# A two-request attention encoder: in the 1024-token request, three heads of four are transposed by DMA instead of one of two, and every product with V stands two slots behind its head

## The chip, the cores and the metric

One core of one Trainium2 chip runs the whole program in one launch. The metric is the device time of that launch in microseconds; lower is better. The engines have these names here: PE is TensorE, DVE is VectorE, ACT is ScalarE, POOL is GpSimd, and SP is the queue (SyncE) from which all DMAs of this kernel are issued.

## What is computed

Two layers of a hybrid attention block, for two requests that share the weights: 512 tokens and 1024 tokens, 1024 channels wide.

```python
for l in range(2):                                   # layers
    shift, scale, gate = split(silu(c) @ w_ada[l] + b_ada[l])
    h = rms_norm(x) * (1 + scale) + shift
    q_lat, kv_lat, k_rope, z_a, q_b, k_b, v_b, z_b = split(h @ w_in[l])
    # group A: 8 heads of latent attention, q and k 96 wide, v 64 wide
    # group B: 8 query heads over 2 key heads, 64 wide, rotated by row and column
    ya = softmax(qa @ ka.T * s_a) @ va * silu(z_a)
    yb = softmax(qb @ kb.T * s_b) @ vb * silu(z_b)
    x = x + gate * (concat(ya, yb) @ w_out[l])
y = rms_norm(x)
```

There is no mask: in the 1024-token request every query row has 1024 scores in each of 16 heads.

## The kernel before

**Tiles and heads.** The program runs four instances one after the other (layer 0 with 512 tokens, layer 0 with 1024, then both of layer 1). An instance first makes all keys and values, then goes over tiles of 128 query tokens: `over_tiles` calls `tile(i, first, last)` on every engine, and a tile has 16 slots, one for each head `h`. The 1024-token instances have 8 tiles, i = 0 to 7. Only these instances are touched by the change.

**One head.** TensorE makes the scores (128 x 1024, two PSUM banks; `scores`). VectorE takes the row maximum (`row_max`), ScalarE the exponential into a row buffer of 32-bit numbers (`exponentials`, two such buffers, for even and odd heads). The product with V needs the probabilities with keys on the partitions, so they have to be transposed, and as two 16-bit parts (high, low) whose sum stands for the 32-bit number. There are two ways:

- by TensorE (odd heads before): `turn` makes 8 transposes of 128 x 128 into two PSUM banks, ScalarE copies each bank out as the high part and VectorE subtracts it from the bank for the low part (`move_pt` on either engine). The result lies in `PT_next`.
- by DMA (even heads before): ScalarE writes the high part of the rows and VectorE the low part (`row_low`) into one buffer `p_rows` of 128 x 2048 16-bit numbers, and SP issues one transposing DMA (`turn_rows`) into `PT`. In the profile `p_rows` has the name of the tile it lies in, `hT`, and `PT` and `probs` lie in `region`.

`mix(h)` is the product with V: 24 matmuls of 64 columns. SP issues the transposing DMA of head h only when the low part of its rows is there and when `mix(h - 2)` has read `PT` (`pv_done`).

**What sets the order.** Each engine runs its own program in the order in which it is written, and waits on semaphores. Besides the head's own steps a slot carries pieces of the projections, placed by hand in the tables `GATE_A`, `FINISH`, `OWN` and `PREPARE`: left of the bar a piece stands ahead of the products, right of it behind them. `"z_b/0"` and `"z_b/1"` are the halves of one projection.

```python
FINISH = [..., {2: "| y_b^T", 11: "| out0/0", 12: "out0/1 |", 13: "| out1/0", 14: "out1/1 |"}]
GATE_A = {0: "| z_a/0", 1: "z_a/1 |"}
OWN = [..., {2: "q_b^T0 |", 3: "| z_b/0", 4: "z_b/1 |", 5: "q_b^T1 |", 15: "| y_a^T"}]
PREPARE = [..., {6: "| q_lat", 7: "| q_b/0", 8: "q_b/1 | q_lat^T", 9: "q_up0 |", 10: "| q_up1", 12: "| q_a^T0", 14: "| q_a^T1"}]
```

All these pieces but `q_b^T0` go through one PSUM bank (`SIDE`), so a piece waits until VectorE has emptied the bank of the piece before it. In slot h TensorE makes the scores of head h + 2, ScalarE the exponential of head h + 1, VectorE the maximum of head h + 2 and the low part of head h + 1. TensorE's order in a slot is: `turn(h)` if h is odd; scores; the pieces left of the bar; in even slots `mix(h - 2)` and `mix(h - 1)`; the pieces right of the bar. VectorE's `outputs(0, i)` (heads 0 to 7 times the gate) stands in slot 8, `outputs(1, i - 1)` in slot 0 of the next tile. SP loads the next tile's rows of h (`load_h`) once `z_b` is done, behind the transposing DMA of head 4. ScalarE's sums of squares for `q_b` follow its work on head 10 in slot 9 (`query_squares`).

## Time and profile before

| | |
|---|---|
| median of 3 runs | 2256.93 us (2255.62 to 2258.09) |
| the profiled execution | 2250.96 us, its span 2248.9 us |
| granted TensorE clock, mean of the span | 0.967 |
| TensorE busy | 1983.3 us (88%) |
| VectorE busy | 1582.6 us (70%) |
| ScalarE busy | 1031.7 us (46%) |
| GpSimd busy | 844.0 us (38%) |
| the DMA queue's packets, share of 16 engines | 40.1% |

The profile is of one execution; its time is 6 us under the median of the runs, so a sum made from it is compared with 2250.96 us and then carried over. Busy shares are means over stages with different limits.

### The profile page before, as it was taken

The page shows a single profiled execution, that of the slowest core. Times are in us where ns is not written, and L with a number is a line of the kernel's source. Part 1 is how long each engine was busy: PE and PEld are TensorE (multiplying, and loading weights), DVE is VectorE, ACT ScalarE, POOL GpSimd, SP SyncE. Part 2 cuts the span into 40 slices and gives each one's busy share as a digit, 9 for nine tenths or more (in the row PEclk, how much of TensorE's full clock was granted, in tenths as well). Part 3 has the DMA queues.
Part 4 walks back from the last instruction along what each step waited for, and adds up shares of the span by engine and source line. Part 5 has one row for each costly group of instructions (what it writes and reads, how often), then busy time and mean ns, then how long its engine had stood idle before and what let it go on. Part 6 is the DMA issues. An engine that isn't in the chain of part 4 may idle for free.

```text
span 2248.9 us, 40514 instructions
## 1 busy us (share of the span) xinstructions
PE 1983.3 (88%) x15994; PEld 1173.9 (52%) x15994; DVE 1582.6 (70%) x2634; ACT 1031.7 (46%) x2110; POOL 844.0 (38%) x1343
## 2 busy tenths in 40 slices
PE   4889998898799999999868899889879999999987
PEld 1445554454456565655534555445446555556553
DVE  4668666586877777777736765748778777777774
ACT  1224345344655555555512434525365555555552
POOL 0663241385531233133136533218752343233320
PEclk7999999998999999999989999999999999999998
DMA  9812124552534443443562001246244334443443
GB/s 330 311 48 76 57 104 171 203 201 48 122 76 85 85 67 76 92 85 68 117 238 94 20 17 69 105 166 257 66 122 95 78 84 80 91 85 76 85 85 85
DMA packets 344752, 248.48 MB, mean 110 GB/s; under 512 B 273418, under 2 KB 299120, under 8 KB 344564
## 3 DMA queue, kind: packets, MB, share of 16 engines
q1 hardware_dynamic: 344566, 245.91, 40.1%
q8 instruction: 128, 2.10, 0.4%
q14 instruction: 58, 0.48, 0.1%
HBM read 130.50 MB, written 39.88 MB: 76 GB/s over the span
## 4 chain that ended last, share of the span: by engine, by line
PE 55%; DVE 20%; DMA 13%; ACT 6%; issue 2%; SPq 2%; POOL 1%; DVEq 0%; ACTq 0%; POOLq 0%
PE psum L737 27%; DMA region<-hT 9%; PE psum L728 6%; PE psum L730 6%; PE psum L729 6%; PE psum L719 5%; PE psum L968 4%; DVE nmax L1370 3%; DVE hT L1076 2%; DMA hT<-h_transposed 2%; DVE hT L1393 2%; DVE region L1386 2%; ACT junk L1487 1%; ACT hT L1619 1%; DVE region L1321 1%
## 5 line engine op out<-in xcount | busy, mean ns | idle before, releaser
L1370 DVE TENSOR_REDUCE nmax<-psum 128x1 f32<-128x1024 f32 (+1 forms) x384 | 399.1, 1039 | 19.2 <-PE psum L737 15.8
L719 PE MATMUL psum<-ident,region 128*128 128x128 f32 (+2 forms) x2200 | 311.0, 280 | 74.1 <-ACT region L1613 30.3
L719 PEld LDWEIGHTS psum<-ident,region 128*128 128x128 f32 (+2 forms) x2200 | 246.6, 141 | 127.2 <-issue 56.7
L1625 ACT ACTIVATE PT_next<-psum 128x512 f16<-128x512 f32 x256 | 140.7, 595 | 322.8 <-PE psum L719 322.5
L737 PE MATMUL psum<-KTa,region 96*128 96x512 f16 x960 | 249.3, 392 | 18.1 <-DVE region L1254 13.6
L1680 POOL TENSOR_TENSOR region<-region,rope_sb 128x64 f32<-128x64 f32 (+3 forms) x384 | 162.8, 445 | 271.3 <-DVE region L1326 261.3
L737 PE MATMUL psum<-Wq,hT 128*128 128x512 f32 (+1 forms) x512 | 202.6, 542 | 0.0
L1386 DVE TENSOR_TENSOR PT_next<-psum,PT_next 128x512 f16<-128x512 f32 x256 | 164.3, 683 | 50.1 <-ACT PT_next L1625 49.9
L728 PE MATMUL psum<-Wq,hT 128*128 128x512 f16 (+1 forms) x512 | 181.3, 354 | 17.4 <-DVE region L1339 10.1
L737 PE MATMUL psum<-KTb,region 128*128 128x512 f16 x640 | 171.5, 383 | 18.5 <-ACT xn L1613 13.1
L730 PE MATMUL psum<-Wq,hT 128*128 128x512 f16 (+1 forms) x512 | 180.9, 353 | 0.0
L729 PE MATMUL psum<-Wq,hT 128*128 128x512 f16 (+1 forms) x512 | 180.8, 353 | 0.0
L1487 ACT ACTIVATE junk<-region 128x64 bf16<-128x64 f32 (+3 forms) x300 | 87.5, 295 | 192.5 <-DVE region L1272 121.7
L1613 ACT ACTIVATE region<-psum,nmax,scalars 128x1024 f32<-128x1024 f32 (+1 forms) x128 | 126.4, 988 | 106.8 <-DVE nmax L1373 105.2
L1613 ACT ACTIVATE region<-psum,nmax,unscale 128x1024 f32<-128x1024 f32 (+1 forms) x128 | 126.1, 985 | 102.0 <-DVE nmax L1373 101.5
L1393 DVE TENSOR_TENSOR hT<-xn,hT 128x1024 f16<-128x1024 f32 x112 | 142.8, 1275 | 38.7 <-ACT hT L1619 36.6
L737 PE MATMUL psum<-region,hT 128*128 128x416 f32 x384 | 150.1, 547 | 20.0 <-DVE hT L1076 17.9
L1619 ACT ACTIVATE hT<-xn 128x1024 f16<-128x1024 f32 x112 | 118.5, 1058 | 101.8 <-DMA region<-hT 100.8
L1680 POOL TENSOR_TENSOR scalars<-scalars 128x1 f32<-128x1 f32 x32 | 6.1, 214 | 418.9 <-ACT region L1613 418.9
L737 PEld LDWEIGHTS psum<-KTa,region 96*128 96x128 f16 x960 | 92.7, 100 | 124.1 <-issue 29.8
L737 PEld LDWEIGHTS psum<-Wq,hT 128*128 128x128 f32 x512 | 93.6, 190 | 75.3 <-issue 71.7
L1321 DVE SCALAR_TENSOR_TENSOR region<-region,psum 128x512 f32<-128x512 f32 x48 | 33.0, 688 | 136.2 <-ACT region L1594 136.2
(202 smaller groups left out, 3883.1 us busy)
## 6 DMA issues: line engine op xcount, KB each, us to landing
w_in_parts<-parts SPq DMA_DIRECT2D x28, 512.0 KB, 2.8
Wq<-w_in_parts SPq DMA_DIRECT2D x16, 896.0 KB, 7.1
Wq<-in_w_in SPq DMA_DIRECT2D x6, 2048.0 KB, 14.9
hT<-h_transposed SPq DMA_DIRECT2D x24, 512.0 KB, 4.3
Va<-in_w_ada SPq DMA_DIRECT2D x12, 1024.0 KB, 5.5
Wout<-in_w_out SPq DMA_DIRECT2D x4, 2048.0 KB, 10.2
h_transposed<-parts SPq DMA_DIRECT2D x16, 512.0 KB, 2.9
Wout<-in_w_out SPq DMA_DIRECT2D x16, 512.0 KB, 4.9
```

Of the source, the lines that this page charges most:

```text
L719: return nc.tensor.transpose(out, in_, ident[0:n, 0:n])
L728: nc.tensor.matmul(out, rows[:, 0, k, :], high(k), start=k == 0, stop=False)
L729: nc.tensor.matmul(out, rows[:, 0, k, :], low(k), start=False, stop=False)
L730: last = nc.tensor.matmul(out, rows[:, 1, k, :], high(k), start=False, stop=k == KD - 1)
L737: last = nc.tensor.matmul(out, lhsTs[k], rhss[k], start=k == 0, stop=k == n - 1)
L1370: last = nc.vector.reduce_max(nmax[:, h:h + 1], scores_buf(h, S), AX_X, negate=True)
L1386: nc.vector.tensor_tensor(pt(h, S, 1, 4 * c)[:, 0:4, :], psum[:, turn_bank(S, h, c), :].rearrange("p (c n) -> p c n", c=4), pt(h, S, 0, 4 ...
L1393: nc.vector.tensor_tensor(p_rows[:, S:2 * S], probs_buf(h, S, i == NT - 1), p_rows[:, 0:S], ALU.subtract).then_inc(s["p_low"], 1)
L1613: nc.scalar.activation(probs_buf(h, S, i == NT - 1), scores_buf(h, S), ACT.Exp, bias=nmax[:, h:h + 1], scale=scale, accum_out=sums[:, h:h ...
L1619: nc.scalar.activation(p_rows[:, 0:S], probs_buf(h, S, i == NT - 1), ACT.Copy).then_inc(s["p_high"], 1)
L1625: nc.scalar.activation(pt(h, S, 0, 4 * c)[:, 0:4, :], psum[:, turn_bank(S, h, c), :].rearrange("p (c n) -> p c n", c=4), ACT.Copy).then_in ...
L1680: mul = lambda out, a, b: nc.gpsimd.tensor_tensor(out, a, b, ALU.mult)
```

## The change

In every tile of a 1024-token instance but the first (i > 0), the heads with h % 4 != 3 are transposed by DMA, 12 of 16; in the first tile it stays with the even heads. Even heads go into `PT`, odd ones into `PT_next`, and each has its own semaphore (`p_turned0`, `p_turned1`). The row buffers alternate between `p_rows` and half of `parts` (`rows_buf`), so ScalarE waits for the transposing DMA two back, not for the last one. TensorE makes `mix(h - 2)` in every slot: ahead of `turn(h)` where head h is TensorE's, else behind the scores and the pieces left of the bar. `outputs(0, i)` moves to the start of slot 9 and `outputs(1, i - 1)` to the start of slot 1 of the next tile.

```diff
+    def by_dma(r, i, h):
+        return r and (h % 4 != 3 if i else h % 2 == 0)
...
+        def rows_buf(h, i):
+            return parts[:, 0, :] if i and dma_heads(1, i, h) % 2 else p_rows
...
                     sp.wait_ge(s["p_low"], row_heads(q, i, h))
                     wait(sp, "pv_done", heads(b0, i, h - 2))
-                    sp.dma_start_transpose(PT[:, :, :, :].rearrange("p a c n -> p (a c) n"), p_rows).then_inc(s["p_turned"], 16)
+                    sp.dma_start_transpose((PT, PT_next)[h % 2][:, :, :, :].rearrange("p a c n -> p (a c) n"), rows_buf(h, i)).then_inc(s[f"p_turned{h % 2}"], 16)
...
-                        if r and h % 2 == 0:
+                        if by_dma(r, i, h):
                             turn_rows(h, i)
...
                     for h, (before_mix, after_mix) in enumerate(slots(first, last, q == 0, r)):
-                        if short or h % 2:
+                        late = not short and not first
+                        if late and not by_dma(r, i, h):
+                            mix(h - 2, i)
+                        if not by_dma(r, i, h):
                             turn(h, i)
...
-                        if not short and h % 2 == 0 and (h or not first):
+                        if late and by_dma(r, i, h) or not short and first and h % 2 == 0 and h:
                             mix(h - 2, i)
-                        if (short or h % 2 == 0) and (h or not first):
+                        if (short or first and h % 2 == 0) and (h or not first):
                             mix(h - 1, i)
...
-                            by_pe = h % 2
+                            by_pe = not by_dma(r, i, h)
+                            if not first and h == 1:
+                                outputs(1, i - 1)
+                            if not first and h == HEADS + 1:
+                                outputs(0, i)
...
-                    if r and h % 2 == 0:
+                    if by_dma(r, i, h):
 
                         act.wait_ge(s["exp_done"], heads(b0, i, h))
-                        wait(act, "p_turned", 16 * (row_heads(q, i, h) - 1))
-                        nc.scalar.activation(p_rows[:, 0:S], probs_buf(h, S, i == NT - 1), ACT.Copy).then_inc(s["p_high"], 1)
+                        k = dma_order.index((i, h))
+                        if k:
+                            wait(act, *rows_turned(q, *dma_order[k - 1 - (k > HEADS)]))
+                        if k == HEADS:
+                            act.wait_ge(s["out_moved0"], 16 * (KD // 2) * (l + 1))
+                        nc.scalar.activation(rows_buf(h, i)[:, 0:S], probs_buf(h, S, i == NT - 1), ACT.Copy).then_inc(s["p_high"], 1)
```

The order of instructions at three places shows what moves. All are of layer 0, 1024 tokens, in a tile from the middle; `psum<-Va,region` and `psum<-Vb,region` are products from `PT`, the same from `PT_next` are products from `PT_next`.

TensorE, from the products of slot 8 to the scores of slot 11, before: the products of heads 6 and 7, `q_lat^T` (2) and `turn(9)` (8) in one row, scores, `q_up0`, scores, the products of heads 8 and 9, `q_up1`, `turn(11)`, scores:

```order
L968 MATMUL psum<-Va,region 128x64 x24
L968 MATMUL psum<-Va,PT_next 128x64 x24
L719 MATMUL psum<-ident,region 128x128 x10
L737 MATMUL psum<-KTb,region 128x512 x4
L737 MATMUL psum<-Wuq,region 128x384 x2
L737 MATMUL psum<-KTb,region 128x512 x4
L968 MATMUL psum<-Vb,region 128x64 x24
L968 MATMUL psum<-Vb,PT_next 128x64 x24
L737 MATMUL psum<-Wuq,region 128x384 x2
L719 MATMUL psum<-ident,region 128x128 x8
L737 MATMUL psum<-KTb,region 128x512 x4
```

The same place now:

```order
L991 MATMUL psum<-Va,region 128x64 x24
L742 MATMUL psum<-ident,region 128x128 x2
L760 MATMUL psum<-KTb,region 128x512 x4
L760 MATMUL psum<-Wuq,region 128x384 x2
L991 MATMUL psum<-Va,PT_next 128x64 x24
L760 MATMUL psum<-KTb,region 128x512 x4
L991 MATMUL psum<-Vb,region 128x64 x24
L760 MATMUL psum<-Wuq,region 128x384 x2
L991 MATMUL psum<-Vb,PT_next 128x64 x24
L742 MATMUL psum<-ident,region 128x128 x8
L760 MATMUL psum<-KTb,region 128x512 x4
```

The 8 transposes of head 9 are gone and the four products stand in four slots, each two behind its head; `turn(11)` stays.

VectorE at the border of two tiles, before, from `outputs(1, i - 1)` in slot 0 to `y_b^T` of slot 2 (a `PT_next` row is `move_pt(1)`, the `xn,hT` row the low part of head 2, `nmax<-psum` a maximum):

```order
L1400 TENSOR_TENSOR region<-psum,region 128x512
L1386 TENSOR_TENSOR PT_next<-psum,PT_next 128x512 x2
L1370 TENSOR_REDUCE nmax<-psum 128x1
L1373 TENSOR_SCALAR nmax<-nmax,scalars 128x1
L1321 SCALAR_TENSOR_TENSOR region<-region,psum 128x512
L1237 TENSOR_REDUCE scalars<-region 128x1
L1393 TENSOR_TENSOR hT<-xn,hT 128x1024
L1333 CAST region<-psum 128x512
L1370 TENSOR_REDUCE nmax<-psum 128x1
L1373 TENSOR_SCALAR nmax<-nmax,scalars 128x1
L1338 CAST region<-psum 128x512
L1339 TENSOR_TENSOR region<-psum,region 128x512
```

The same place now, from the low part of head 1 in slot 0:

```order
L1419 TENSOR_TENSOR hT<-region,hT 128x1024
L1427 TENSOR_TENSOR region<-psum,region 128x512
L1396 TENSOR_REDUCE nmax<-psum 128x1
L1399 TENSOR_SCALAR nmax<-nmax,scalars 128x1
L1347 SCALAR_TENSOR_TENSOR region<-region,psum 128x512
L1263 TENSOR_REDUCE scalars<-region 128x1
L1419 TENSOR_TENSOR parts<-xn,parts 128x1024
L1359 CAST region<-psum 128x512
L1396 TENSOR_REDUCE nmax<-psum 128x1
L1399 TENSOR_SCALAR nmax<-nmax,scalars 128x1
L1364 CAST region<-psum 128x512
L1365 TENSOR_TENSOR region<-psum,region 128x512
```

`move_pt(1)` is gone, a low part of head 1 is new, and `outputs(1, i - 1)` with the maximum of head 3 behind it now stands directly ahead of the gate `z_a` (the `SCALAR_TENSOR_TENSOR` row).

SP over most of a tile, before, from the load of x in slot 2 (the transposes of heads 4, then 6 to 14, then 0 and 2 of the next tile, then x again):

```order
L636 DMA region<-in_x_sample 128x1024
L662 DMA_TRANSPOSE region<-hT 128x16x128
L563 DMA hT<-h_transposed 128x2048
L662 DMA_TRANSPOSE region<-hT 128x16x128 x5
L639 DMA x_after_layer_1<-region 128x1024
L662 DMA_TRANSPOSE region<-hT 128x16x128 x2
L636 DMA region<-in_x_sample 128x1024
```

Now, from the same load to the store of the tile's result:

```order
L659 DMA region<-in_x_sample 128x1024
L685 DMA_TRANSPOSE region<-hT 128x16x128
L586 DMA hT<-h_transposed 128x2048
L685 DMA_TRANSPOSE PT_next<-parts 128x16x128
L685 DMA_TRANSPOSE region<-hT 128x16x128
L685 DMA_TRANSPOSE region<-parts 128x16x128
L685 DMA_TRANSPOSE PT_next<-hT 128x16x128
L685 DMA_TRANSPOSE region<-parts 128x16x128
L685 DMA_TRANSPOSE region<-hT 128x16x128
L685 DMA_TRANSPOSE PT_next<-parts 128x16x128
L685 DMA_TRANSPOSE region<-hT 128x16x128
L662 DMA x_after_layer_1<-region 128x1024
```

Between the load of h and the store stand eight transposing DMAs (heads 5, 6, 8, 9, 10, 12, 13, 14) in place of five.

## Rows read from the trace of the kernel before

**Rows 1.** Page, groups: line engine op, out<-in, count | busy us, mean ns | idle before.

```profile
L1625 ACT ACTIVATE PT_next<-psum 128x512 f16<-128x512 f32 x256 | 140.7, 595 | 322.8 <-PE psum L719 322.5
L1386 DVE TENSOR_TENSOR PT_next<-psum,PT_next 128x512 f16<-128x512 f32 x256 | 164.3, 683 | 50.1 <-ACT PT_next L1625 49.9
L1393 DVE TENSOR_TENSOR hT<-xn,hT 128x1024 f16<-128x1024 f32 x112 | 142.8, 1275 | 38.7 <-ACT hT L1619 36.6
L1619 ACT ACTIVATE hT<-xn 128x1024 f16<-128x1024 f32 x112 | 118.5, 1058 | 101.8 <-DMA region<-hT 100.8
```

**Rows 2.** Windows, layer 0, 1024 tokens: length, busy of PE, PEld, DVE, ACT, POOL, PEclk.

```profile
651.20:1075.80 424.60, 405.74 (x4049) 251.36 (x4046) 324.69 (x465) 231.91 (x440) 127.81 (x178) 1.00 0.41 79
```

**Rows 3.** SP's timeline: head 4's transposing DMA, first and last of seven, of six.

```profile
632.30 1.98 SPq L662 DMA_TRANSPOSE region<-hT  x1
...
1075.81 1.92 SPq L662 DMA_TRANSPOSE region<-hT  x1
...
1721.27 2.91 SPq L662 DMA_TRANSPOSE region<-hT  x1
...
2101.48 1.93 SPq L662 DMA_TRANSPOSE region<-hT  x1
```

**Rows 4.** Line L662: time of the 128 transposing DMAs from issue to landing.

```profile
DMA to landing us min/median/max: 4.2/4.3/5.9
```

**Rows 5.** TensorE's timeline, one tile of layer 0: start, us, what [idle before].

```profile
705.69 0.86 PE L968 MATMUL psum<-Va,region 128*128 128x64 f16 x24
...
707.09 1.07 PE L719 MATMUL psum<-ident,region 128*128 128x128 f32 x8
707.99 1.46 PE L737 MATMUL psum<-KTa,region 96*128 96x512 f16 x6
...
712.91 0.27 PE L728 MATMUL psum<-Wq,hT 128*128 128x256 f16 x1 [0.39 <-DMA hT<-h_transposed]
...
724.01 0.86 PE L968 MATMUL psum<-Va,PT_next 128*128 128x64 f16 x24
...
733.00 1.09 PE L719 MATMUL psum<-ident,region 128*128 128x128 f32 x8 [1.21 <-ACT region L1613]
...
758.51 0.39 PE L728 MATMUL psum<-Wq,hT 128*128 128x512 f16 x1
...
772.77 0.39 PE L728 MATMUL psum<-Wq,hT 128*128 128x512 f16 x1 [0.69 <-DVE region L1339]
```

**Rows 6.** The chain in the same tile: start, us, what.

```profile
708.52 4.26 DMA hT<-h_transposed
...
724.27 4.43 DMA region<-hT
...
728.78 1.06 ACT hT L1619
```

**Rows 7.** VectorE's timeline at the border of the next tile.

```profile
760.88 0.68 DVE L1400 TENSOR_TENSOR region<-psum,region 128x512 f32<-128x512 f32 x1
...
766.87 0.69 DVE L1321 SCALAR_TENSOR_TENSOR region<-region,psum 128x512 f32<-128x512 f32 x1 [1.82 <-ACT region L1594]
...
769.93 1.21 DVE L1370 TENSOR_REDUCE nmax<-psum 128x1 f32<-128x1024 f32 x1
771.18 0.21 DVE L1373 TENSOR_SCALAR nmax<-nmax,scalars 128x1 f32<-128x1 f32 x1
```

**Rows 8.** Layer 1, the same border: TensorE's timeline at `z_a/0`.

```profile
1849.81 0.39 PE L728 MATMUL psum<-Wq,hT 128*128 128x512 f16 x1
```

**Rows 9.** The chain there: head 0's transposing DMA, and `z_b/0`.

```profile
1853.35 4.99 DMA region<-hT
...
1866.07 0.39 PE psum L728
```

**Rows 10.** The chain in layer 0's last tile: head 4's transposing DMA, and `turn(11)`.

```profile
1075.81 5.50 DMA region<-hT
...
1097.05 1.09 PE psum L719 x8
```

More of the change, by code:

```diff
@@ L1434, in tile @@
                                 next_max(h, i, last)
-                        if h == HEADS:
+                        if (short or first) and h == HEADS:
                             outputs(0, i)
-                        if h == 0 and not first:
+                        if short and h == 0 and not first:
                             outputs(1, i - 1)
@@ L1631, in tile @@
                     for h, names in enumerate(schedule):
-                        if not short and h % 2:
+                        if not short and not by_dma(r, i, h):
                             move_pt(h, i)
```

55 lines of the change are left out of this document (35 added, 20 removed).

## The prediction, made before the changed kernel was run

> T(h) is the transposing DMA of head h; a prime marks a head of the next tile. Times inside a tile are in us.
>
> **What bounds the kernel now.** The page's busy shares come first: TensorE looks like the bound. The windows over six 1024-token tiles of layer 0 make it sharper: TensorE 405.7 busy of 424.6 (96%), VectorE 76%, ScalarE 55%, all at full clock [rows 2]. By that view every matmul taken out is time won. So I looked next at where in a tile TensorE's end is set by TensorE, and where a chain through other engines ends at the same moment. SP's timeline gives the length of a middle tile: T(4) is issued at 632.30 and, six tiles on, at 1075.81, 73.9 a tile; in layer 1 at 1721.27 and, five on, at 2101.48, 76.0 a tile [rows 3]. TensorE's timeline cuts a tile at five points [rows 5]:
>
> - A, `mix(2)` 705.69 to `q_lat` 712.91: 7.2.
> - B, `q_lat` to the end of `mix(6)`, 724.01: 11.1.
> - C, from there to `turn(11)`, 733.00: 9.0.
> - D, `turn(11)` to `z_a/0`, 758.51: 25.5.
> - E, `z_a/0` to `z_b/0`, 772.77: 14.3. In layer 1 it is 1849.81 to 1866.07, 16.3 [rows 8, 9]. From `z_b/0` to the next `mix(2)` nothing moves.
>
> A, C and E end in a wait: `q_lat` for the load of h, `turn(11)` for ScalarE, `z_b/0` for VectorE [rows 5]. The waits are short, 0.4 to 1.2, because TensorE's own work is nearly as long as the chains. That is what the 96% hides.
>
> **The change part by part.** *Removed:* heads 1, 5, 9 and 13 of seven tiles in two layers, 56 `turn`s of 8 transposes. One takes TensorE 707.09 to 707.99, 0.9 [rows 5], so 3.6 a tile and 50 in all if nothing else ended the segments. Each also takes two copies of 0.595 from ScalarE and two subtractions of 0.683 from VectorE, and adds one of 1.058 and one of 1.275 [rows 1]: 0.1 less on either engine, counted as nothing. What the segments do:
>
> A holds `turn(5)`. SP issues T(4) when `mix(2)` is done, then the load of h at 708.52, which lands 4.26 later, at 712.78 [rows 6]. Neither SP's order nor `mix(2)` moves, so `q_lat` still starts 7.2 after `mix(2)`. T(4) lands in 4.3 [rows 4], so `mix(4)` ends some 6.1 after `mix(2)` began, inside it. TensorE loses `turn(5)` and `mix(5)` here and waits longer. Change 0.
>
> B now holds `mix(5)`, 0.7 (two products fill 705.69 to 707.09 [rows 5]): **+0.7**, since B is TensorE's own work from end to end.
>
> C holds `turn(9)`. T(8) is issued at 724.27, as `mix(6)` ends, lands 4.43 later; ScalarE's copy for head 10 waits for it (728.78), and behind that copy in ScalarE's order stand the sums of squares and head 11's exponential, for which `turn(11)` waits at 733.00 [rows 5, 6]. With two row buffers the copy for head 10 waits for the DMA two back, and in the new order 8, 9, 10 that is again T(8). So the 9.0 stay, without `turn(9)` in them. T(9) is new: `mix(7)` ends some 3.1 after `mix(6)`, T(9) lands 4.3 + 0.4 later, `mix(9)` is over at 8.5, just inside. Change 0.
>
> D loses `turn(13)` (0.9) and `mix(15)` (0.7, to the next segment). But the pieces go through one PSUM bank: `q_a^T0`, `out1/0`, `q_a^T1` and `z_a/0` each come closer behind the piece whose bank VectorE must empty, and the exponential of head 0' still follows `turn(15)`. The bounds are 0 and -1.6; stepping through the pieces I find 1.2 of it eaten: **-0.4**.
>
> E holds `turn(1')` and ends in VectorE's chain. Before, `z_a` starts on VectorE at 766.87 [rows 7], 8.4 after `z_a/0`, and `z_b/0` comes 5.9 later. Now `outputs(1)` stands ahead and waits for `mix(15)`, which ends behind `z_a/1`: 8.4 less about 1.0 of tanh and signals, less `turn(1')` 0.9, plus 0.7, is 7.2. Then 0.2 of signal, `outputs` 0.7 [rows 7], the maximum of head 3', held up behind it, 1.2 + 0.2 [rows 7]: `z_a` starts at 9.4 to 9.5, and `z_b/0` follows at 15.3. **+1.0** in layer 0. T(1'), which waits for `mix(15)`, gives 7.2 + 0.2 + 4.3 + 0.2, then `mix(1')`, `turn(3')` and 1.3 of scores: 14.8, just inside. In layer 1 SP issues T(0') only behind the store of the finished tile, 3.5 after `z_a/0`, it lands 5.0 later [rows 8, 9], ScalarE's copy for head 2' waits for it and the tanh stands behind that copy: this chain is untouched and longer than VectorE's new one, so E stays at 16.2: change **-0.1**.
>
> The last tile has no pieces for a next one, so chains set it: T(4) 1075.81 to `turn(11)` 1097.05, 21.2 [rows 10]. Here T(5) comes in behind T(4) on the DMA queue, head 8's copy waits for it, T(8) and T(9) follow; I get some 22.4, and 0.8 back from `turn(13)` behind it: +0.4 a layer.
>
> *Sum:* E 7 x 1.0 - 7 x 0.1 = +6.3; B 12 tiles x 0.7 = +8.4; D 12 x -0.4 = -4.8; last tiles +0.8: **+11**. 2250.96 + 11 = 2262 for an execution like the profiled one, and with the median 6 above it, **2268**.
>
> *A price weighed.* A transposing DMA moves 16 blocks of 128 x 128 16-bit numbers in 4.3 from issue to landing, at most 5.9 [rows 4], which is 0.27 a block.
> The Trainium skill (VectorE: DVE Perf Modes, Rules for kernel authors) says to transpose 128 x 128 on TensorE where PSUM will do as the destination, by the DMA crossbar otherwise, which speaks against this change. Its table gives 1309 ns a block by DMA; 16 in a row would be 20.9 us a head by its figure, 251 us for 12 heads, and the tile would be three times as long. The trace does not agree, with 4.3 us a head, so this has no chance of its own.
>
> **The rivals.** *TensorE was the bound (faster).* If the chains of A, C and E shrink with TensorE's work, the 50 are kept: 2250.96 - 50, median 2207; with half of them 2232. For it: 96% busy and short waits. Against it: each of the three chains holds a DMA or an engine order that the change leaves as it is. It decides where a chain in A, C, E is more than 1 shorter than I have it; at C, T(8) to landing would have to take under about 3.
> The Trainium skill (Advanced Engine Details and Errata, X-Bar Transpose) expects 350 to 400 GB/s of a transposing DMA; the 512 KB would then take 1.3 to 1.5 us, an estimate from that page, and chain C would end under TensorE's work. The trace's least is 4.2 us from issue to landing; it does not agree for the whole way. Chance 0.2, mostly for a step of mine that is too long.
>
> *The tile border costs nothing (same).* If VectorE's new order at E is hidden in layer 0, the sum is +11 - 7 = +4: 2261. For it: `z_b/0` waited only 0.7. Chance 0.18.
>
> *The transposes get in each other's way (slower still).* T(1'), T(5), T(9) are within 0.5 of the paths, and 5.9 occurs where DMAs overlap [rows 4]. 1.6 more at T(1') gives +1.2 in E, at T(9) +1.1 to 1.4 in C, at T(4) and the load of h +0.4 in A: 3 a tile, 13 tiles, +38: 2306 at most, 2280 to 2290 at half. Chance 0.2.
>
> *My sum.* Chance 0.42; its own range is 2260 to 2278.
>
> **How the numbers follow.** Two times of this kernel closer than 0.2% (4.5 us) can't be told apart. Slower by more: 0.42 + 0.2, less a little at the lower edge, 0.6. Within: 0.18. Faster: 0.22. The range goes from 2244, some way into the faster case, to 2292, three fifths of the way into the bound for contention. This leaves 0.2 out, most of it below.
>
> **What the changed profile would show.** Right: TensorE's busy share falls by about 50 us and its idle time rises by 60; no `turn` but of heads 3, 7, 11, 15 in tiles 1 to 7; `q_lat` still about 7.2 after `mix(2)`, waiting 2 for the load of h; `turn(11)` still 9.0 after `mix(6)`, waiting for ScalarE; `z_b/0` about 15.3 after `z_a/0` in layer 0, with VectorE idle for `mix(15)` ahead of it; 184 transposing DMAs, median landing 4.3 to 4.5; a middle tile of 75.2 in layer 0 and 76.2 in layer 1. Wrong: tiles of 70 to 72 (TensorE bound), or landings above 5 with TensorE waiting for T(1'), T(5) or T(9) for more than 1 (contention).

## The result, and the profile after

The changed kernel takes 2309.27 us (median of 4 runs, 2307.37 to 2315.78); the kernel before took 2257.51 beside it. The ratio is 1.0236, 95% interval 1.0216 to 1.0256: **52 us slower**. The forecast was 2268 with a range of 2244 to 2292; the direction is right, the size is not, and the time lies outside the range.

| | before | after |
|---|---|---|
| the profiled execution | 2250.96 us | 2315.78 us |
| its span | 2248.9 us | 2313.7 us |
| granted TensorE clock, mean | 0.967 | 0.954 |
| DMA queue's packets, share of 16 engines | 40.1% | 46.2% |

The two profiled executions lie 65 us apart, the medians 52: before's is 6.5 us under its median, after's 6.5 over its own. So sums from the two traces come out some 13 us (0.9 a tile) too high in all.

The top of the page of the changed kernel, and what answers to [rows 1]: ScalarE's copies (L1659) and VectorE's low parts (L1419), one row for each pair of buffers.

```profile
PE 1981.7 (86%) x15546; PEld 1153.7 (50%) x15546; DVE 1584.7 (68%) x2578; ACT 1033.2 (45%) x2054; POOL 874.2 (38%) x1343
...
L1665 ACT ACTIVATE PT_next<-psum 128x512 f16<-128x512 f32 x144 | 79.4, 594 | 202.3 <-PE psum L742 201.9
...
L1412 DVE TENSOR_TENSOR PT_next<-psum,PT_next 128x512 f16<-128x512 f32 x144 | 93.4, 685 | 61.0 <-ACT PT_next L1665 60.7
```

```profile
L1659 ACT ACTIVATE hT<-xn 128x1024 f16<-128x1024 f32 x64 | 67.6, 1057 | 125.4 <-DMA region<-hT 124.3
...
L1659 ACT ACTIVATE parts<-xn 128x1024 f16<-128x1024 f32 x48 | 50.7, 1057 | 96.7 <-DMA region<-parts 92.9 <-issue 3.1
```

The copies and subtractions of one PSUM bank into `PT_next` went from 256 to 144, two fewer for each of the 56 heads, at an unchanged 594 and 685 ns. New is how long ScalarE's copies into the buffers of rows wait for transposes: 124 + 93 us, where it was 101 [rows 1].

The same stretch of layer 0 as in [rows 2], same columns:

```profile
651.20:1075.80 424.60, 378.79 (x3665) 225.70 (x3663) 305.04 (x416) 220.37 (x401) 136.77 (x177) 0.98 0.52 100
```

TensorE works 379 of 424.6 us instead of 406, in a window that no longer holds six tiles. The third number from the end is the granted clock, and it is new too: 0.98 where it was 1.00. In layer 1, 1721 to 2101, it is 0.95, before 1.00.

TensorE's waits in the changed kernel (what, on what, total us, times, longest):

```profile
PE psum L991 <- DMA region<-hT: 38.5, 21, 3.8
PE psum L991 <- DVE region L1412: 31.9, 49, 1.4
PE psum L991 <- DMA PT_next<-hT: 27.2, 20, 2.5
...
PE psum L751 <- DMA hT<-h_transposed: 17.0, 12, 2.2
```

Products (L991) wait 66 us for transposes in these rows alone; in the same list of the kernel before it is 17.5. `q_lat` waits 17.0 for the load of h, before 5.0. All 184 transposing DMAs, to be set beside [rows 4]:

```profile
  ACT hT L1659: 142.1, 36
  ACT parts L1659: 101.3, 28
  PEld psum L991: 93.4, 57
  PE psum L991: 80.7, 55
...
DMA to landing us min/median/max: 4.2/4.3/7.3
```

The median is 4.3, as forecast; the maximum is not, and 60 of the 184 land after more than 5 us (33 of 128 before). One tile shows where the late ones sit. TensorE's timeline, the same tile as [rows 5]:

```profile
717.33 0.86 PE L991 MATMUL psum<-Va,region 128*128 128x64 f16 x24
...
722.58 0.87 PE L991 MATMUL psum<-Va,region 128*128 128x64 f16 x24 [1.31 <-DMA region<-hT]
724.90 0.27 PE L751 MATMUL psum<-Wq,hT 128*128 128x256 f16 x1 [1.45 <-DMA hT<-h_transposed]
...
746.49 0.87 PE L991 MATMUL psum<-Vb,PT_next 128*128 128x64 f16 x24 [1.90 <-DMA PT_next<-hT]
...
772.88 0.39 PE L751 MATMUL psum<-Wq,hT 128*128 128x512 f16 x1 [0.18 <-DVE region L1365]
```

SP's timeline there: T(4), the load of h, T(5), T(6); then T(8), T(9), T(10).

```profile
718.29 1.76 SPq L685 DMA_TRANSPOSE region<-hT  x1
720.11 1.14 SPq L586 DMA_DIRECT2D hT<-h_transposed  x1
721.35 3.55 SPq L685 DMA_TRANSPOSE PT_next<-parts  x1
725.00 1.90 SPq L685 DMA_TRANSPOSE region<-hT  x1
736.98 1.83 SPq L685 DMA_TRANSPOSE region<-parts  x1
740.41 1.70 SPq L685 DMA_TRANSPOSE PT_next<-hT  x1
744.13 2.79 SPq L685 DMA_TRANSPOSE region<-parts  x1
```

And the chain: T(9) takes 6.03 from issue to landing, and `mix(9)` waits for it; T(12) takes 5.91, and the chain runs on through a copy and a low part (head 14's) into a maximum.

```profile
740.41 6.03 DMA PT_next<-hT
746.49 0.87 PE psum L991 x24
...
755.95 5.91 DMA region<-hT
...
761.95 1.06 ACT hT L1659
...
763.03 1.23 DVE hT L1419
```

What the clock does shows in layer 1, at T(4) of tile 1. Windows of the changed kernel, columns as in [rows 2]; `mix(4)` is the second, the first half of `q_lat` the third, the rest the fourth:

```profile
1767.60:1770.70 3.10, 0.04 (x1) 0.00 (x0) 2.01 (x4) 0.00 (x0) 0.00 (x0) 0.98 1.09 177
1770.70:1772.20 1.50, 1.46 (x24) 1.31 (x24) 0.35 (x1) 1.44 (x2) 0.00 (x0) 0.50 1.10 324
1772.20:1774.00 1.80, 1.76 (x9) 1.26 (x10) 1.80 (x2) 0.81 (x2) 0.73 (x4) 0.50 0.74 167
1774.20:1776.50 2.30, 2.30 (x41) 2.14 (x39) 0.71 (x3) 0.00 (x0) 2.22 (x2) 1.00 1.08 202
```

TensorE idles for 3.1 us, since T(4) lands 6.05 after its issue. Then the granted clock reads 0.50, the 1.2 GHz level, over the next 3.3 us: `mix(4)` takes 1.46 instead of 0.86, and the matmuls of `q_lat` come every 0.21 us instead of every 0.11.

The segments of the prediction, from the starts of the same matmuls in each tile of the traces (mean over tiles i = 1 to 5 of the layer; F is `z_b/0` to the next tile's `mix(2)`, and A follows it, so it is that of tiles 2 to 6):

```
                B      C      D      E     F     A    tile
before  L0    11.10   8.92  25.52  14.26  6.49  7.49  73.78
        L1    11.10   8.94  25.55  16.27  6.49  7.62  75.97
after   L0    12.52   9.76  25.25  15.99  6.53  7.84  77.90
        L1    13.38   9.82  25.26  16.79  6.53  7.98  79.78
```

A tile is 4.1 us longer in layer 0 and 3.8 in layer 1. B, C and E carry it. The 24 matmuls of `q_lat`, with which B begins, took 2.62 us in all ten of these tiles before. Now they take 2.62 in three and 3.4 to 5.0 in seven, 3.12 in the mean of layer 0 and 4.09 in that of layer 1. In one of the three, B is long all the same, 12.8, because `mix(5)`, right behind `q_lat`, waits for T(5):

```profile
805.58 0.87 PE L991 MATMUL psum<-Va,PT_next 128*128 128x64 f16 x24 [0.78 <-DMA PT_next<-parts]
```

E has its long tiles too. In tile 3 of layer 0 it is 18.6: T(1') lands after 5.56, and behind the wait for it the granted clock reads 0.50 (862.66 to 869.00). `mix(1')`, `turn(3')` and the scores behind it take 5.6 in all, where they take 2.9 at 784.60, one tile earlier:

```profile
863.45 1.46 PE L991 MATMUL psum<-Va,PT_next 128*128 128x64 f16 x24 [2.19 <-DMA PT_next<-hT]
864.72 1.95 PE L742 MATMUL psum<-ident,region 128*128 128x128 f32 x8
866.46 2.77 PE L760 MATMUL psum<-KTa,region 96*128 96x512 f16 x6
```

### The profile page after: what moved, and what is told of

Read it like the earlier page. It is cut to its first block, busy times and chain, and to the rows that moved or that the text cites. A ratio compares the mean times of both kernels' runs of the same rounds, so it can differ in the third digit from the quotient of the medians.

```text
span 2313.7 us, 39559 instructions
## 1 busy us (share of the span) xinstructions
PE 1981.7 (86%) x15546; PEld 1153.7 (50%) x15546; DVE 1584.7 (68%) x2578; ACT 1033.2 (45%) x2054; POOL 874.2 (38%) x1343
## 3 DMA queue, kind: packets, MB, share of 16 engines
q1 hardware_dynamic: 461046, 275.28, 46.2%
## 4 chain that ended last, share of the span: by engine, by line
PE 54%; DVE 22%; DMA 14%; ACT 4%; SPq 2%; issue 2%; POOL 1%; DVEq 0%; ACTq 0%; POOLq 0%
PE psum L760 27%; PE psum L751 6%; PE psum L752 6%; PE psum L753 6%; PE psum L742 5%; PE psum L991 4%; DVE nmax L1396 4%; DMA PT_next<-hT 4%; DMA region<-hT 3%; DMA hT<-h_transposed 2%; DVE hT L1102 2%; DMA region<-parts 2%; DVE region L1412 2%; DVE hT L1419 1%; SPq L685 1%
## 5 line engine op out<-in xcount | busy, mean ns | idle before, releaser
L742 PE MATMUL psum<-ident,region 128*128 128x128 f32 (+2 forms) x1752 | 268.1, 288 | 62.6 <-ACT region L1649 13.8
L760 PE MATMUL psum<-KTa,region 96*128 96x512 f16 x960 | 253.3, 397 | 20.0 <-DVE region L1280 13.5
L742 PEld LDWEIGHTS psum<-ident,region 128*128 128x128 f32 (+2 forms) x1752 | 201.7, 144 | 107.7 <-issue 45.1
L751 PE MATMUL psum<-Wq,hT 128*128 128x512 f16 (+1 forms) x512 | 188.0, 367 | 27.5 <-DMA hT<-h_transposed 17.0
L752 PE MATMUL psum<-Wq,hT 128*128 128x512 f16 (+1 forms) x512 | 186.9, 365 | 0.0
L753 PE MATMUL psum<-Wq,hT 128*128 128x512 f16 (+1 forms) x512 | 186.3, 364 | 0.0
L1665 ACT ACTIVATE PT_next<-psum 128x512 f16<-128x512 f32 x144 | 79.4, 594 | 202.3 <-PE psum L742 201.9
L1412 DVE TENSOR_TENSOR PT_next<-psum,PT_next 128x512 f16<-128x512 f32 x144 | 93.4, 685 | 61.0 <-ACT PT_next L1665 60.7
L991 PE MATMUL psum<-Va,region 128*128 128x64 f16 x2304 | 90.5, 195 | 48.6 <-DMA region<-hT 26.4
L1733 POOL TENSOR_TENSOR rinv<-stat,eps 128x1 f32<-128x1 f32 (+1 forms) x96 | 27.7, 289 | 273.0 <-ACT junk L1519 272.1
L991 PE MATMUL psum<-Vb,region 128*128 128x64 f16 x2304 | 92.9, 197 | 38.7 <-DMA region<-hT 12.1
```

What stands on the lines that cost most here:

```text
L742: return nc.tensor.transpose(out, in_, ident[0:n, 0:n])
L751: nc.tensor.matmul(out, rows[:, 0, k, :], high(k), start=k == 0, stop=False)
L752: nc.tensor.matmul(out, rows[:, 0, k, :], low(k), start=False, stop=False)
L753: last = nc.tensor.matmul(out, rows[:, 1, k, :], high(k), start=False, stop=k == KD - 1)
L760: last = nc.tensor.matmul(out, lhsTs[k], rhss[k], start=k == 0, stop=k == n - 1)
L991: last = nc.tensor.matmul(out, pt(h, S, a, c)[:, 0, :], v, start=c == 0 and a + b == 0, stop=c == NT - 1 and a == 1)
```

## The experiments

All are edits of the changed kernel. Each ratio is to the kernel before on the same chip.

### VectorE's order at the border

```diff
-                            if not first and h == 1:
-                                outputs(1, i - 1)
-                            if not first and h == HEADS + 1:
-                                outputs(0, i)
...
                                 next_max(h, i, last)
+                            if not first and h == 1:
+                                outputs(1, i - 1)
+                            if not first and h == HEADS + 1:
+                                outputs(0, i)
```

Expected:

> The changed kernel with outputs(1, i - 1) and outputs(0, i) one place later on VectorE, behind the maximum of their slot. Theory 'order' (the tile border is set by VectorE's chain behind mix(15)): in layer 0 z_b/0 comes 14.8 to 15.0 us after z_a/0 instead of 15.3 in undisturbed tiles, the limit then being T(1') behind mix(15), so at most 0.5 us x 7 tiles; q_up1 no longer waits 0.8 us for its bank, but turn(11) still waits for ScalarE. Together 3 to 6 us less than 2309. Rival (the border costs nothing, all of the 52 us is late transposes): no change within 0.2%. If the border were the main cost: 15 us or more.

Measured: 2313.9 us, ratio 1.0241 (1.0220 to 1.0261). E in layer 0 fell from 15.99 to 15.44 (in undisturbed tiles from 15.34 to 14.63), D rose from 25.25 to 25.92. The order at the border is worth 0.5 where it stands, and D takes it back.

### The new order without the new DMAs

```diff
-        return r and (h % 4 != 3 if i else h % 2 == 0)
+        return r and h % 2 == 0
```

> The changed kernel with only the even heads by DMA in all tiles: the new order of products and outputs without the 56 new transposing DMAs. By the chains: VectorE at the tile border now has outputs, move_pt(1) and the maximum of head 3 behind mix(15), which itself ends one turn later; z_b/0 some 17 us after z_a/0 in layer 0 (14.3 before) and in layer 1 (16.3 before); elsewhere as before. That is +2.7 x 7 + 1 x 7 = +26 us: 2280 to 2290. Theory 'the DMAs do the harm': close to 2257, the 52 us being all of the transposes. Theory 'the order does the harm': 2300 or more.

Measured: 2256.42 us, ratio 0.9984 (0.9971 to 0.9997), a hair faster than before. The order costs nothing; **the 56 heads that go by DMA instead of by TensorE cost all of the 52 us.** My forecast for this run was wrong. Its segments show how it comes out nearly even:

```
                B      C      D      E     F     A    tile
order   L0    12.16   8.46  25.85  14.99  6.49  7.53  75.48
alone   L1    12.16   8.46  25.83  14.99  6.49  7.57  75.50
```

B has the +0.7 of `mix(5)` (its least is 11.8) and a slow `q_lat` in one tile of five, D has +0.3, E +0.7 in layer 0; C is 0.5 shorter. In layer 1, E fell from 16.27 to 14.99: with two buffers of rows the copy for head 2' waits for the transpose two back, which is T(14) here, instead of T(0'), so the chain behind the late T(0') [rows 9] is gone from this run. In the changed kernel T(1') stands between, and the transpose two back is T(0') again. In the last tiles T(4) to `turn(11)` takes 18.6 and 18.9 where it took 21.2 and 21.3. The two traces by themselves would put the order 7 us above the kernel before (2257.66 against a profile that was fast for its kernel), the medians beside each other 3 below.

### No load of h, and the load first

```diff
                             sp.wait_ge(s["mm_ready"], n)
                             if i == 0:
                                 sp.wait_ge(s["h_stored1"], 8 * (b0 + NT))
-                            load_h(i + 1)
+                            if not r:
+                                load_h(i + 1)
```

> The changed kernel without the loads of h for query tiles 1 to 7 of the 1024-token instances: each tile uses the rows of h of tile 0, so a part of the computation's input is left out. Theory 'neighbours' (T(4) and T(5) are slowed by the load of h between them, transposes alone do not slow each other): T(5) lands in 4.3 us instead of 5.5 to 7.3, mix(5) does not wait, and q_lat starts 6.1 us after mix(2) instead of 7.9, set by T(4). 2.4 us a tile, some 13 tiles: 2309 - 31 = 2278. Theory 'pairs' (two transposes in flight slow each other): T(5) still lands late, only q_lat's wait goes: 2309 - 20 = 2289.

The tiles of the 1024-token instances work on stale h here. Measured: 2292.56 us, ratio 1.0153 (1.0124 to 1.0182), 17 us less than with the load. T(5), which lands after 5.8 (median of 14) in the changed kernel, lands after 4.5 here. That is less than either theory gave: A is 1.4 shorter, but E stays long (16.1 and 16.6).

The second edit only exchanges the two on SP:

```diff
-                        if by_dma(r, i, h):
+                        if h != 4 and by_dma(r, i, h):
                             turn_rows(h, i)
...
                         for name in names:
                             side(name, owner(name, i))
+                        if h == 4 and by_dma(r, i, h):
+                            turn_rows(h, i)
```

> The changed kernel with the load of h issued ahead of T(4) instead of behind it, at the moment z_b is done. The load is issued some 2.6 us earlier; T(4) leaves SP 0.3 to 0.5 us later and then has the load as a neighbour, landing in 5.5 instead of 4.3; q_lat is then set by mix(4), 7.3 to 7.7 us after mix(2) instead of 7.9; T(5) lands in 4.3 to 5 instead of 5.5 to 7.3, so mix(5)'s wait goes (0.7 us a tile). Together -0.9 us x 13: 2309 - 12 = 2297. If the load is as costly wherever it stands: 2305 to 2313.

Measured: 2312.45 us, ratio 1.0232 (1.0208 to 1.0256), no change. T(5) now lands after 4.5 in the median of 14, but T(4), 4.3 before, after 5.5 (5.1 to 7.5). A transpose that is issued while the load of h is in flight is late by 1 to 3 us, whichever it is.

### Half of each transpose

```diff
-    sp.dma_start_transpose((PT, PT_next)[h % 2][:, :, :, :].rearrange("p a c n -> p (a c) n"), rows_buf(h, i))
+    sp.dma_start_transpose((PT, PT_next)[h % 2][:, :, :, :].rearrange("p a c n -> p (a c) n") if i == 0 else (PT, PT_next)[h % 2][:, 0, :, :],
+                           rows_buf(h, i) if i == 0 else rows_buf(h, i)[:, 0:SMAX])
```

> The changed kernel in which the transposing DMAs of tiles 1 to 7 carry only the high half of the rows, 256 KB instead of 512; the low parts of those tiles' probabilities are left out (old ones are read in their place). All instructions and waits stay. Theory 'late transposes' (the 52 us are waits for transposing DMAs): they land in 3.0 to 3.3 us instead of 4.3, and every segment that ends in one gets about 1 us shorter: C 1, B 0.7 to 1, E 1 in layer 1, A 0.3: 3 us a tile, 13 tiles: 2309 - 40 = 2270. Rival (fixed costs of issuing on SP, or ScalarE's and VectorE's order, set the path): within 10 us of 2309.

Only the high parts are transposed in tiles 1 to 7; all else is done, with stale low parts. Measured: 2247.39 us, ratio 0.9941 (0.9918 to 0.9964), 62 us less than the changed kernel. The rows of line L685 there:

```profile
  PE psum L992: 27.7, 20
...
DMA to landing us min/median/max: 3.0/3.1/6.8
```

With 1.2 less from issue to landing, products wait 28 instead of 81 us. So the time from issue to landing stands on the path, and not the number of instructions or their order. It does not say which part of that time: SP's own share of it fell too, from 1.9 to 1.23 us. And it shortens the transposes of the even heads as well, so its 62 us are not to be set against the 52. The segments are 74.02 and 74.54 a tile, E 15.3 and 15.8, C 8.5.

### One odd head at a time

```diff
-        return r and (h % 4 != 3 if i else h % 2 == 0)
+        return r and (h % 2 == 0 or i and h == 13)     # and 5, 1, 9, 11; 13 and 15; 11 and 13
```

> The new order with the even heads and head 13 by DMA in tiles 1 to 7 (9 of 16), to be held against the new order with the even heads alone, 2256.4. Head 13's transpose has projections all around it. Per-head theory: D gets 0.6 us shorter, as in the changed kernel (25.25 against 25.85), nothing else moves: -8, 2248. If every added DMA costs, wherever it stands: +13 (a quarter of the 52), 2269.

> The new order with the even heads and head 5 by DMA in tiles 1 to 7. T(5) is issued right behind the load of h; it lands in 5.5 us or more and mix(5) waits for it in slot 7, while turn(5) stood under q_lat's wait for the load anyway. +0.7 to +1.5 a tile, 14 tiles: 2266 to 2277. If the place does not matter: 2269, as for head 13.

> The new order with the even heads and head 1 by DMA in tiles 1 to 7. T(1) waits for mix(15) and stands on the path of the tile border: E was 15.0 in both layers with the even heads alone, and 16.0 and 16.8 with head 1 (and 5, 9, 13) by DMA. +1.4 on average, 14 tiles: 2276. If head 1 costs only through the other added DMAs around it: 2256.

> The changed kernel with by_dma true for the even heads and head 9 alone (in tiles 1 to 7): the last of the four heads that the change adds. If the four heads' costs add up (heads 5, 1, 13 alone gave +32, +20 and -5 us against the order alone, all four +53), head 9 costs about +6 us: 2262 us. If costs grow with the number of transposes in flight or with the missing slack of neighbours, the four alone add up to less than 53, and head 9 alone costs nothing or gains: 2245 to 2257 us.

> Even heads and head 11 by DMA in tiles 1 to 7. With 13 alone 2251.7, with 11 and 13 2245.2, with neither 2256.4 us. If the two add up, head 11 alone gives 2249 to 2251 us; if head 11 gains only where head 13 keeps TensorE ahead, 2254 to 2257 us.

| odd heads by DMA | us | ratio (95%) | against the order alone |
|---|---|---|---|
| none | 2256.42 | 0.9984 (0.9971 to 0.9997) | |
| 13 | 2251.7 | 0.9964 (0.9951 to 0.9976) | -5 |
| 11 | 2259.32 | 0.9987 (0.9972 to 1.0002) | +1, by the ratios |
| 1 | 2276.98 | 1.0077 (1.0056 to 1.0099) | +20 |
| 9 | 2280.67 | 1.0091 (1.0076 to 1.0105) | +24 |
| 5 | 2288.81 | 1.0123 (1.0090 to 1.0155) | +32 |
| 1, 5, 9, 13 | 2309.27 | 1.0236 (1.0216 to 1.0256) | +53 |

The four alone add up to 71, together they cost 53 (by the ratios, each to the kernel before on its own chip, 72 and 57): each lateness hides part of the next. The losses are where the prediction had a segment end in a chain. Head 1: E 15.76 and 16.69 instead of 14.99; 1.0 of layer 1's 1.7 is in its undisturbed tiles too (16.01), where T(0') is again the transpose for which the copy for head 2' waits. Head 9: C 9.83 instead of 8.46. Head 5: B 13.06 and 13.23 instead of 12.16, of which 0.6 and 0.7 are a slower `q_lat` (3.55 and 3.69 in the mean, 2.95 in the order alone) and 0.3 the wait of `mix(5)` for T(5), A +0.4. With 13, with 1 and with 11 and 13 `q_lat` takes 2.62 in every one of the ten tiles. Head 13 lies in D, where TensorE sets the end, and D falls from 25.85 to 25.21. Head 11 alone gains nothing; next to head 13 it gains some 7 us, as the next run shows.

### Two odd heads in D

> The changed kernel with the even heads, 11 and 13 by DMA in tiles 1 to 7. The products that follow heads 10 to 13 are the long ones (D, 25 us), in which TensorE is the busy engine. Theory 'a head gains where its transpose lands ahead of its product': TensorE loses 1.07 us of turning a tile, 14 tiles, so 2236 to 2248 us. Rival as for 13 and 15: 2260 us or more.

Measured: **2245.23 us, ratio 0.9934 (0.9921 to 0.9947), faster than both kernels**, by 0.7% and by 3%. C and D together take 33.4 and 33.6 where the order alone has 34.3. Landings are no better than elsewhere, but products wait 23 us for them instead of 81:

```profile
  PE psum L991: 23.3, 25
...
DMA to landing us min/median/max: 4.2/4.3/6.9
```

> Even heads, 11 and 13 by DMA, and outputs() behind the maximum of the slot on VectorE (the order in which the kernel before has them). In the kernel that was changed this moved 0.55 us out of E and gave it back in D. Theory 'E is bound by VectorE's chain ahead of z_b/0': up to 0.5 us a tile, 2238 us. Rival 'given back in D': 2243 to 2248 us.

Measured: 2246.76 us, ratio 0.9938 (0.9919 to 0.9957), the same. E is 14.99 in both.

> The changed kernel with the even heads, 13 and 15 by DMA in tiles 1 to 7. Head 13 alone gained 5 us against the order alone. T(15) stands between T(14) and the next tile's T(0), near no load of h but next to the loads of x and the store. Theory 'a head gains where its transpose lands ahead of its product': 2240 to 2250 us. Rival 'every transpose that follows another in 3.4 us costs where nothing but it bounds the chain of exponentials': 2260 to 2275 us.

Measured: 2312.14 us, ratio 1.0240 (1.0222 to 1.0258), a loss of 60 us against 13 alone, and for a reason that neither theory had. Layer 0 is unharmed (74.66 a tile). In layer 1, E takes 22.7. SP's timeline at the border, T(12), T(13), T(14), the load of the gains, the store of the finished tile, T(15), T(0'):

```profile
1862.55 1.91 SPq L685 DMA_TRANSPOSE region<-parts  x1
1865.98 1.80 SPq L685 DMA_TRANSPOSE PT_next<-hT  x1
1872.31 1.74 SPq L685 DMA_TRANSPOSE region<-parts  x1
1874.10 1.20 SPq L669 DMA_DIRECT2D region<-in_g_final  x1
1882.04 0.34 SPq L672 DMA_DIRECT2D out<-region  x1
1882.48 3.20 SPq L685 DMA_TRANSPOSE PT_next<-hT  x1
1885.78 1.81 SPq L685 DMA_TRANSPOSE region<-parts  x1
```

The store waits on SP for the rows of the finished tile, until 1882.04, and T(15) stands behind it. I had read this very queue for T(0') [rows 9] and did not ask what it does to a T(15).

### Why some transposes land late

> The changed kernel, and behind every transposing DMA of SP a copy of 256 bytes from DRAM to DRAM (one row of the input to a scratch tensor that nothing reads). Theory 'anything else between two transposes holds the second up': as with the records of instruction fetches, a transpose that follows another within 4 us lands after 5.4 to 5.6 instead of 4.3 us; two or three more late landings in every tile, about +2 us a tile, 2330 to 2350 us. Rival 'only size counts' (the load of h is slow for its 512 KB or so, the fetches for something else that goes with them): landings as in the changed kernel, 2305 to 2315 us, at most SP's extra issue time of about 1 us where two transposes are 3.4 us apart.

> As the run with copies of 256 bytes, but each copy has 16 KB, the size of the one packet of an instruction fetch, which the trace shows on one of the 16 DMA engines for 0.9 to 1.8 us. SP issues as much as in that run (2351 us), so the two are to be compared. Theory 'a transpose ends with the slowest of its engines, and a long packet on one of them holds the next transpose up': the second transpose of each close pair (heads 1, 5, 9, 13 behind heads 0, 4, 8, 12; 2, 6, 10, 14 behind those) lands after 5 us or more nearly every time, and the time is well above 2351 us, 2370 to 2400. If the copy is split into small packets over the engines: 4.3 to 4.8 us and 2350 to 2365. Rival 'the fetch is a mark of something else': landings as in the run with 256 bytes, median 4.3 us, 2351 us.

```diff
+    scratch = nc.dram_tensor("scratch", (400, 64), F32, kind="Internal").ap()
...
     sp.dma_start_transpose((PT, PT_next)[h % 2][:, :, :, :].rearrange("p a c n -> p (a c) n"), rows_buf(h, i)).then_inc(s[f"p_turned{h % 2}"], 16)
+    n = row_heads(q, i, h)
+    sp.dma_start(scratch[n:n + 1, :], x_sample[0, 0:1, 0:64]).then_inc(s["scratch_done"], 16)
```

The second has rows of 4096 numbers. Measured: 2351.2 us (1.0403, 1.0386 to 1.0420) with 256 bytes and 2331.94 (1.0315, 1.0291 to 1.0339) with 16 KB. The time with 256 bytes is near what its first theory gave, the reason is another: landings over 5 us number 60 of 184 in the changed kernel, 60 with 256 bytes and 59 with 16 KB. What grew is SP's issuing. The 256-byte run, T(4), a copy, the load of h, T(5):

```profile
717.91 1.87 SPq L686 DMA_TRANSPOSE region<-hT  x1
...
720.95 0.57 SPq L587 DMA_DIRECT2D hT<-h_transposed  x1
721.63 4.24 SPq L686 DMA_TRANSPOSE PT_next<-parts  x1
```

The load goes out 3.0 after T(4)'s issue instead of 1.8 (a copy takes SP 1.0 in the median of either run), and `q_lat` waits for it:

```profile
726.18 0.27 PE L754 MATMUL psum<-Wq,hT 128*128 128x256 f16 x1 [3.10 <-DMA hT<-h_transposed]
```

And behind that wait the clock falls again: `q_lat` takes 4.3 us in the mean there and B is 13.5 to 13.6. The 16 KB did not test a long packet: the page counts the same 466,934 packets on the queue in both runs, so the copy was cut up, as its expectation allowed for. That it is the faster of the two I can't explain.

What does mark the late ones is a count over the traces of all kernels but the one with half transposes and the two with copies (tiles 1 to 7). "Fetch" is a packet that the trace calls an instruction packet and that starts 0.9 to 4.4 us behind the issue of the transpose; "other DMA" is a load or store in flight at some time between issue and landing:

```
fetch  other DMA   transposes   median us   over 5 us
no     no             884         4.25          9
no     yes            586         4.28        114
yes    no             502         5.17        277
yes    yes            310         5.47        232
```

With neither neighbour 1 in 100 is late, with a fetch 6 in 10. The page has 124 of the large fetches (q8):

```profile
q8 instruction: 124, 2.03, 0.4%
```

They have 16 KB each, and one packet takes 1.0 us (median) and up to 1.8. The trace shows more of how the two meet. A transposing DMA raises its semaphore in 16 steps. Of T(9) at 740.41, 14 steps come by 4.45 and the last two at 5.07 and 6.03; a 16 KB packet starts 3.98 behind its issue and takes 0.96. Of T(12) at 755.95, 15 steps come by 4.35 and the last at 5.91; its packet starts at 3.89. T(1') at 857.85, with a packet at 3.04, has all 16 steps late, 5.41 to 5.56. So a packet near the end holds up one or two parts of sixteen, an earlier one all of them. But for the fetches this is a correlation and an argument; only the load of h was moved and taken away. In the kernel before, 33 of 128 transposes land after more than 5 us too, but T(8), on which C hangs, never does (4.7 at most in 14 tiles; in the changed kernel 5 of 14 do). The fetches fall where they fall: no run controls that.

### The waits filled with matmuls

```diff
+                        fill = r and i and h == 6 and not last
+                        if fill:
+                            wait(pe, "pt_low", turned(q, i, 2) + 1)
+                            for _ in range(10):          # 20 in the second
+                                transpose(psum[:, T_BANK, 0:P], ident[:, :])
                         if late and by_dma(r, i, h) or not short and first and h % 2 == 0 and h:
                             mix(h - 2, i)
+                        if fill:
+                            for _ in range(8):
+                                transpose(psum[:, T_BANK, 0:P], ident[:, :])
```

> The changed kernel, and in slot 6 of tiles 1 to 6 TensorE transposes the identity (128x128, 0.11 us each) 10 times ahead of mix(4) and 8 times ahead of q_lat, into a PSUM bank that is free then. Nothing reads them; they take the place of idle time (1.3 and 1.4 us in most tiles). In the changed kernel q_lat's 24 matmuls take 2.6 us in only 3 of the 12 tiles looked at and 3.4 to 5.1 in the others, where the granted clock reads 0.50 behind the two waits; in the kernel before they take 2.6 in all ten middle tiles. Theory 'the waits for T(4) and h let the clock fall, and that is most of what B lost beyond 0.7': q_lat back at 2.6 us in most tiles, B about 11.8 to 12.2, 2290 to 2298 us. Rival 'the clock falls for another reason, the waits only go with it': q_lat as long as before, and the fillers add up to 0.4 us a tile: 2309 to 2316 us.

> The same with 20 transposes ahead of mix(4). Where T(4) lands in time this delays mix(4) by about 1 us, but the load of h, for which q_lat waits 1.4 us more, hides it. Where T(4) is late the whole wait of 3.1 us is filled but for 0.8. Theory 'idle time lets the clock fall': q_lat at 2.6 us in all tiles, 2288 to 2298 us. Rival: 2310 to 2320 us.

Measured: 2300.37 us (1.0194, 1.0170 to 1.0219) with 18 and **2292.30 us (1.0151, 1.0133 to 1.0170) with 28 matmuls of no use**, 9 and 17 us faster than without them. The windows of the second, the same two stretches:

```profile
651.20:1075.80 424.60, 392.74 (x3866) 240.53 (x3865) 312.69 (x426) 224.11 (x406) 142.72 (x181) 1.00 0.54 103
1721.00:2101.00 380.00, 348.29 (x3427) 213.44 (x3425) 282.39 (x384) 203.81 (x365) 126.06 (x158) 1.00 0.55 107
```

The clock stays at 1.00. `q_lat` takes 2.62 us in every one of the twelve tiles of either run; what B has above 11.8 (it is 12.0 to 12.2) is `mix(5)` waiting for T(5). So the waits do lower the clock. In the changed kernel's trace the granted clock reads 0.50 for 78 us of tiles 1 to 7, with 18 matmuls for 21 and with 28 for 14, in the kernel before for 3. The 17 us are what that is worth, less what the matmuls of no use cost; the kernel with 28 of them is still 34 us slower than the one before, and these are the waits themselves and B's +0.7. The last 8 us between the two runs are not from `q_lat`, which is no faster with 28, but E is at its undisturbed 15.3 and 16.0 in the profile of that run, so T(1') was in time; why, I can't say.

## Why the prediction was wrong in size

Two steps failed: that every transpose lands after the median 4.3 us and so "just inside" the chains, and that TensorE's work runs at full clock behind the new waits. Part by part:

**Where TensorE is not the bound.** Right for A, B's start, C and E: TensorE lost 56 `turn`s and the kernel is slower, and the rival with TensorE as the bound is refuted there. In D it is the bound, as heads 11 and 13 show. One check failed: TensorE's busy time was to fall by 50 us and stands at 1981.7 against 1983.3. Of the difference 15 us come with the order (1998.2 in the order alone); for the rest, matmuls at the lower clock count longer, a sign of the clock that I read late.

**A, change 0.** Measured +0.35, and 0 or less when the load of h or half of the transposes is gone (6.4 to 6.6). `q_lat` starts 7.6 after `mix(2)` in the tile shown. "T(4) lands in 4.3 ... inside it" fails where it lands in 6, as at 1764.63 above; in the tile shown it is the load of h, issued at 720.11, that took 4.66.

**B, +0.7.** The term is right as far as it goes: 11.8, the 11.10 of before and 0.7, is what B measures in undisturbed tiles, here and in the runs with head 13, with head 1 and with 11 and 13. In all it was +1.4 and +2.3. Of the rest `q_lat` itself is +0.5 and +1.5 (3.12 and 4.09 against 2.62); `mix(5)`'s wait for T(5) makes the other 0.2 in layer 0 and 0.1 in layer 1. The step that failed is "B is TensorE's own work from end to end": so it is, but it begins behind two waits, and its work runs at the clock that they leave. The prediction had `q_lat` wait 2 and took the clock for granted.

**C, change 0.** This is the step that failed most plainly: "T(9) lands 4.3 + 0.4 later, `mix(9)` is over at 8.5, just inside". The 8.5 were made of 3.1, 4.3 + 0.4 and 0.7; with 6.0 for the landing the same sum gives 10.2. In the tile shown T(9) took 6.03, `mix(9)` waited 1.90, and from T(8)'s issue at 736.98, when `mix(6)` ends, to `turn(11)` at 747.20 it is 10.2. C has 8.8 where the landings are 4.3, and 9.8 in the mean. T(8), from which the 9.0 were built, comes late as well: after 6.0 in tile 3 of layer 0, where C is 10.5.

**D, -0.4.** Measured -0.3.

**E, +1.0 and -0.1.** Both terms are right in undisturbed tiles. In layer 0 these have 15.3, to the tenth what the chain of VectorE gave. In layer 1 they have 16.0, where the prediction had 16.2, and by the chain that it named: in tile 2, with `z_a/0` at 1900.40, T(0') is issued 3.3 later, behind the store, and lands 5.0 after that; ScalarE's copy, the tanh, VectorE and `z_b/0` follow.

```profile
1903.67 5.00 DMA region<-parts
...
1916.40 0.39 PE psum L751
```

The means are 15.99 and 16.79. One tile of five in layer 0 has 18.6 (T(1')), two in layer 1 have 17.1 (T(0') lands after 6.1) and 18.9 (T(1') after 5.8). In the 18.6 and the 18.9 the late landing costs well under 1; some 2.6 are the clock behind it.

**Last tiles, +0.4.** T(4) to `turn(11)` was to take 22.4 and took 23.4 and 22.6 (21.2 and 21.3 before).

**The sum.** +11 us. Two things are missing. The first is the landings: the terms were sized with the median, 4.3, for every transpose. A path that ends in the later of two things pays for each late landing and gets nothing back for a punctual one, so with a third of the landings over 5 us, T(5) in almost every tile, the mean of C, A and E lies above what the median gives: +0.9, +0.4 and, in E, 0.1 to 0.3 a tile. The second is the clock, which the waits for late landings lower: +0.5 and +1.5 in B, +0.5 in E. With `mix(5)`'s wait, these are about 2.6 a tile in layer 0 and 3.5 in layer 1, 43 for 14 tiles, and with the +11 some 54, against 52 between the medians and 65 between the two traces; what the traces have above 54 I have not placed.

My rival "the transposes get in each other's way" named T(1'), T(9), T(4) and the load of h with C, E and A, and bounded them at +38; I gave it 0.2, as if the 5.9 of [rows 4] were an exception. Its name is not quite right: two transposes alone, less than 4 us apart, do not slow each other (249 such, median 4.27, 2 over 5 us). It is the load of h, shown by taking it away, and what comes with instruction fetches, which is not shown. And it, too, left out B and the clock.

**The order's price.** I had the order at +23 to +33 by itself (the expectation above) and it was nil. In layer 0 the chain that I had at 17 for E measured 14.99. In layer 1 and in the last tiles I had not seen that with the even heads alone the second buffer frees the chain of [rows 9] and shortens the one of [rows 10].

**The Trainium skill's rule.** The Trainium skill (VectorE: DVE Perf Modes, Rules for kernel authors) prefers TensorE for 128 x 128 transposes. I had set it aside for its price. The direction it points to came true for heads 1, 5 and 9, though not for the 1309 ns a block of the same page (The three transpose paths): the landings here are 0.27 us a block in the median and 0.46 at the worst (7.3 for 16). For heads 11 and 13 it did not hold.

## What to carry to other kernels

Work that is moved from the busiest engine to a DMA gains only where that engine sets the end of the segment; head by head, the same edit gave -5 and +32 us. Where a product is to come "just inside" a DMA's landing, take the distribution of landings and not the median, and ask for slack of the longest one seen; a wait that TensorE did not have before can cost twice, once by itself and once by the lower clock of the matmuls behind it. And on a queue with loads and stores, ask for each new DMA what stands ahead of it and what that waits for: a store waiting for its data cost 60 us.

## What the hardware showed unexpectedly

- A transposing DMA of 512 KB lands 4.25 us after its issue in the median with nothing beside it (884 of them, 9 over 5 us), and after 5.2 to 5.5 in the median where the trace has an instruction packet in its time. With half of the bytes it is 3.0 to 3.1.
- Behind a load of 512 KB on the same queue it lands after 5.1 to 7.5, and SP needs 3.5 to 3.8 us (median) to issue it instead of 1.9.
- The clock: behind 3.1 us of idle time TensorE's granted clock read 0.50 over the next 3.3 us. 336 matmuls of no use (28 in each of 12 tiles) made the kernel 17 us faster.
- Two transposing DMAs less than 4 us apart cost each other nothing (median 4.27).
